# A two-block transformer kernel on one core: the second block's softmax heads in pairs, mirrored decay levels, meta keys' values over all rows

## The reference, cut to what matters

```python
# block 2, attention: 16 heads of 64; with 256 tokens it is one block, so plain causal softmax
q, k = rope(heads(q)), rope(heads(k))
s = einsum('bhqd,bhkd->bhqk', q, k) * 64 ** -0.5
p = softmax(where(k_pos <= q_pos, s, NEG))
o = einsum('bhqk,bhkd->bhqd', p, v)

# block 2, HGRN2: 8 heads, keys and values of 128, b = running sum of log(forget)
a[t, s] = sum_d q[t, d] * k[s, d] * exp(b[t, d] - b[s, d])      for s <= t
o = a @ v       # and RMSNorm by head, times silu(output gate)

# block 1, attention: two softmaxes a head over 272 keys, of which 16 are meta tokens
a = softmax(s0) - lam * softmax(s1);  o = a @ v
```

## Time and profile before

| | |
|---|---|
| median of 3 executions | 1184.91 us (1183.97 to 1189.07) |
| the profiled execution | 1187.4 us, its span 1185.8 us |
| busy in the span | PE 1141.6, DVE 719.4, ACT 600.0, POOL 649.5 us |
| mean granted TensorE clock | 0.985 of full speed |
| chain that ended last | PE 77%, DVE 11%, issue 6% |
| one heads2 iteration | 65.36 us |

### The profile page before, as it was taken

How to read it: one execution, slowest core, us unless ns; L and a number is a source line. 1 busy time by engine, 2 the same in 40 slices (tenths; PEclk the granted TensorE clock), 3 DMA queues, 4 the chain that set the end, 5 groups by cost and what they waited for, 6 DMA issues and landing times.

```text
span 1185.8 us, 24894 instructions
## 1 busy us (share of the span) xinstructions
PE 1141.6 (96%) x8962; PEld 1095.6 (92%) x8962; DVE 719.4 (61%) x1364; ACT 600.0 (51%) x1112; POOL 649.5 (55%) x451
## 2 busy tenths in 40 slices
PE   6999999999889999999899999999999999999997
PEld 6999999998779999999899989898999989999996
DVE  5675766688656777525875856757666546444322
ACT  5644444455255656437555455555535455444332
POOL 4666666660355666644763637364375436656542
PEclk9999999999889999998999999999999999999998
DMA  8444444341343454543433423333445425545531
GB/s 324 145 147 141 156 141 161 142 147 72 142 178 114 173 192 169 205 148 137 164 126 109 162 99 122 141 109 139 147 174 172 149 90 195 178 177 198 193 143 36
DMA packets 26209, 179.43 MB, mean 151 GB/s; under 512 B 2848, under 2 KB 4128, under 8 KB 4768
## 3 DMA queue, kind: packets, MB, share of 16 engines
q1 hardware_dynamic: 25856, 178.28, 42.2%
q10 hardware_dynamic: 288, 0.27, 0.1%
HBM read 177.49 MB, written 1.05 MB: 151 GB/s over the span
## 4 chain that ended last, share of the span: by engine, by line
PE 77%; DVE 11%; issue 6%; POOL 2%; ACT 2%; DVEq 0%; DMA 0%; POOLq 0%; ACTq 0%
PE ps L570 51%; PE ps L852 10%; PE ps L930 2%; POOL parts L415 2%; PE ps L636 1%; PE ps L485 1%; DVE ps L2185 1%; DVE act L1823 1%; PE ps L667 1%; PE ps L610 1%; DVE branch L1964 1%; PE ps L923 1%; ACT parts L1130 1%; DVE parts L415 1%; PE ps L533 1%
## 5 line engine op out<-in xcount | busy, mean ns | idle before, releaser
L415 POOL TENSOR_TENSOR parts<-ring,parts 128x1024 fp32r<-128x1024 f32 x208 | 513.5, 2479 | 478.2 <-ACT parts L1130 475.1
L570 PE MATMUL ps<-x_high,parts 128*128 128x256 f32 (+2 forms) x3088 | 417.4, 284 | 4.3 <-DVE glu L1999 2.2
L570 PEld LDWEIGHTS ps<-x_high,parts 128*128 128x128 f32 x3088 | 387.2, 189 | 15.1 <-issue 8.1
L1130 ACT ACTIVATE parts<-ring 128x1024 fp32r<-128x1024 f32 x324 | 323.9, 1049 | 138.5 <-PE ps L852 69.3
L415 DVE TENSOR_TENSOR parts<-ring,parts 128x1024 fp32r<-128x1024 f32 x116 | 151.8, 1309 | 127.3 <-ACT parts L1130 127.3
L570 PE MATMUL ps<-x_low,parts 128*128 128x256 f32 (+2 forms) x1520 | 214.5, 284 | 0.0
L570 PEld LDWEIGHTS ps<-x_low,parts 128*128 128x128 f32 x1520 | 196.3, 189 | 0.0
L1750 DVE SCALAR_TENSOR_TENSOR ps<-glu,table_sb,ps 128x256 f32<-128x256 f32 x232 | 93.3, 479 | 0.6 <-DVE ps L1750 0.2
L852 PE MATMUL ps<-act_high,parts 128*128 128x256 f32 x704 | 87.8, 280 | 0.0
L852 PEld LDWEIGHTS ps<-act_high,parts 128*128 128x128 f32 x704 | 85.1, 188 | 0.0
L570 PE MATMUL ps<-parts,x_high 128*128 128x256 f32 x448 | 62.3, 285 | 0.9 <-DVE work L2098 0.9
(11 more groups left out here) (331 smaller groups left out, 1611.0 us busy)
## 6 DMA issues: line engine op xcount, KB each, us to landing
ring<-weights SPq DMA_DIRECT2D x166, 1024.0 KB, 4.8
res<-h_in SPq DMA_DIRECT2D x4, 272.0 KB, 3.7
act<-mem SPq DMA_DIRECT2D x1, 1024.0 KB, 14.9
out<-xT SPq DMA_DIRECT2D x4, 256.0 KB, 2.5
table_sb<-table SPq DMA_DIRECT2D x1, 969.5 KB, 9.0
table_sb<-table ACTq DMA_DIRECT2D x1, 132.5 KB, 3.5
work<-positions ACTq DMA_DIRECT2D x1, 128.0 KB, 4.7
```

Of the source, the lines that this page charges most:

```text
L415: eng.tensor_tensor(parts[:, LOW - HIGH + p, cols], ring[:, slot, cols], parts[:, p, cols].bitcast(F32), ALU.subtract)\
L570: mm = pe.matmul(out, left(k), right(k), start=step_ == 0 and k == 0, stop=step_ == 2 and k == KB - 1)
L1130: sc.activation(parts[:, p, cols], ring[:, slot, cols], ACT.Copy).then_inc(split_high, 1)
```

## The change

**Softmax heads in pairs.** `scores2(s)`, `values2(s)`, `maxima2()`, `exps2()` and `turned2()` now each do two heads, one on either half of the array, with a second `p2` and `p2T` (where the other half of `kl` was). The pair's scores lie in banks 4 and 5, and their transposes go back to the same banks. The matmuls of the two halves alternate. The order of all three queues around them is changed: TensorE does both `turn2` behind `hgrn_scores(1, 0)`; VectorE does `maxima2` for both heads, then `low_v` of chunk 6, then both `normalise2`; ScalarE does `exps2` for both, then `ahead2(4)`. In the second pair VectorE has `low_values`, `level(13)` and `cross_level` between `maxima2` and `normalise2`, and ScalarE has `ahead2(5)` ahead of `decay(13)` and `cross_decay`, which stood ahead of it before.

**Mirrored levels.** The second half's tokens are kept in reverse order of keys, so that the keys of a level in the first half and those in the second take different rows of one 128 x 128 `kl`, and one matmul of 128 columns does both halves. VectorE multiplies the keys of each half by itself (64 columns each, the second written backwards). `iN`'s second half is reversed by a matmul with a reversed identity (`mirror_values`, 256 columns, between tiles 4 and 5) and copied back by ScalarE, which waits for it ahead of `decay(2)`; `head_keys` becomes four copies of half the width. The reversed identity and masks are made by VectorE in `down1` (`mirrored_constants`). GpSimd's clearing of `kl` falls away.

**Meta keys' values.** The matmul over the 16 meta keys takes all 128 rows, the others being cleared once at the start by GpSimd.

```diff
@@ TensorE
-                pe.matmul(ps[:, 7, 0:P], v_meta[0:META, h * P:h * P + P], a1M[0:META, :], start=True, stop=False)
+                pe.matmul(ps[:, 7, 0:P], v_meta[:, h * P:h * P + P], a1M, start=True, stop=False)
...
+            def mirror_values(i):
+                b = STREAM.bank("heads2", 3)
+                hold(pe, bank_read[2], n.before(bank_read[2]))
+                pe.wait_ge(tile_read[b], STREAM.before("heads2", i, 3) + 1)
+                pe.matmul(ps[:, 2, 0:CW], both_diagonals[:, P:2 * P], iN[:, 1, :], start=True, stop=True)\
+                  .then_inc(values_mirrored, 1)
+            def scores2(s):
...
+                for half in range(2):
+                    pe.matmul(ps[:, 4 + half, 0:P], q_r[rows[half], s, 0:P], k_r[rows[half], s, 0:P], start=True, stop=True)
+                for half in range(2):
+                    mm = pe.matmul(ps[:, 4 + half, P:3 * P], q_r[rows[half], s, P:SEQ], k_r[rows[half], s, :], start=True, stop=True)
...
             def level(h, l, bank, at):
-                for blk in range(2):
-                    mm = pe.matmul(ps[:, bank, at + HD * blk:at + HD * blk + HD], kl[:, l, blk * P:blk * P + P],
-                                   ql[:, l, blk * HD:blk * HD + HD], start=True, stop=True)
-                return mm
+                return pe.matmul(ps[:, bank, at:at + P], kl[:, l, :], ql[:, l, :], start=True, stop=True)
...
-                for t in range(6):
+                for t in range(5):
                     proj(t)
+                mirror_values(i)
+                proj(5)
...
                 scores2(0)
                 hgrn_values(0)
                 proj(10)
+                hgrn_scores(1, 0)
                 turn2(0)
-                scores2(1)
-                hgrn_scores(1, 0)
+                turn2(1)
                 proj(11)
                 values2(0)
-                turn2(1)
-                scores2(2)
+                scores2(1)
                 proj(12)
                 hgrn_scores(1, 1)
+                proj(13)
+                turn2(0)
+                turn2(1)
+                hgrn_scores(1, 2)
+                proj(14)
                 values2(1)
-                turn2(2)
-                scores2(3)
-                proj(13)
-                hgrn_scores(1, 2)
-                values2(2)
-                turn2(3)
-                proj(14)
                 hgrn_values(1)
-                values2(3)
                 proj(15)
@@ ScalarE, heads2
+                sc.wait_ge(values_mirrored, n.next(values_mirrored))
+                sc.activation(iN[:, 1, :], ps[:, 2, 0:CW], ACT.Copy).then_inc(bank_read[2], 1)
                 decay(2)
...
-                exps2(0)
+                exps2()
                 ahead2(4)
                 hgrn_output(i, 0)
                 copy2(10, gates[:, i * 2, 0:SEQ], fn=ACT.Tanh, scale=0.5)
                 turned2()
-                exps2(1)
                 for x in range(9, 13):
                     decay(x)
                 copy2(11, gates[:, i * 2 + 1, 0:SEQ], fn=ACT.Tanh, scale=0.5)
-                turned2()
-                exps2(2)
+                output2(i, 0)
+                exps2()
+                ahead2(5)
                 decay(13)
                 cross_decay(i, 1)
-                ahead2(5)
@@ VectorE, level and heads2
-                ve.tensor_tensor(halves(kl[:, l, :], m)[:, :, 0, :], halves(kh[:, i * 2 + h, :], m)[:, :, 0, :],
-                                 e[:, :, 0, :], ALU.mult)
+                ve.tensor_tensor(halves(kl[:, l, :], m)[:, :, 0, :], keys[:, 0:b, 0, :], e[:, 0:b, 0, :], ALU.mult)
+                ve.tensor_tensor(halves(kl[:, l, :], m)[:, ::-1, 1, ::-1], keys[:, b:, 0, :], e[:, b:, 0, :], ALU.mult)
...
-                maxima2(0)
-                normalise2()
+                maxima2()
                 low_v("heads2", i, 6)
-                maxima2(1)
-                normalise2()
+                normalise2(0)
+                normalise2(1)
                 gather0()
                 for x in range(9, 13):
                     level(i, 1, x)
-                maxima2(2)
-                normalise2()
+                maxima2()
+                low_values(i, 0)
                 level(i, 1, 13)
                 cross_level(i, 1)
-                low_values(i, 0)
+                normalise2(0)
+                normalise2(1)
                 low_v("heads2", i, 7)
-                maxima2(3)
-                normalise2()
```

More of the change, by code:

```diff
@@ L362, in blocks_kernel @@
         m_max, m_sum = small[0:LEAD, 16:32], small[0:LEAD, 32:48]
+        nmax2, rsum2, rden2 = (small[:, 16 + 4 * j:20 + 4 * j] for j in range(3))
         lb, one_lb, lb_t = small[:, 48:56], small[:, 56:64], small[:, 64:88]
@@ L895, in rotate @@
                           start=True, stop=True).then_inc(bank_full[2], 1)
[L897 to L900, removed]
-                    pe.wait_ge(roped, n.next(roped, 2))
[L902 to L905, removed]
@@ L907, in turn2 @@
-            def turn2(j):
+            def mirror_values(i):
[5 more added lines that the diff above has]
+            def scores2(s):
+                if s == 0:
+                    pe.wait_ge(roped, n.next(roped, 2))
+                hold(pe, bank_read[5], n.now(bank_read[5]))
+                rows = [slice(HD * half, HD * half + HD) for half in range(2)]
+                for half in range(2):
+                    pe.matmul(ps[:, 4 + half, 0:P], q_r[rows[half], s, 0:P], k_r[rows[half], s, 0:P], start=True, stop=True)
+                for half in range(2):
+                    mm = pe.matmul(ps[:, 4 + half, P:3 * P], q_r[rows[half], s, P:SEQ], k_r[rows[half], s, :], start=True, stop=True)
+                mm.then_inc(bank_full[4], 1)
@@ L908, in turn2, with values2 @@
+            def turn2(half):
+                n.before(bank_read[4])
+                n.before(bank_read[5])
                 pe.wait_ge(probs_ready, n.next(probs_ready))
-                hold(pe, bank_read[5], n.before(bank_read[5]))
                 for b in range(3):
-                    mm = pe.transpose(ps[:, 5, b * P:b * P + P], p2[:, b * P:b * P + P], ident)
+                    mm = pe.transpose(ps[:, 4 + half, b * P:b * P + P], p2[half][:, b * P:b * P + P], ident)
                 mm.then_inc(bank_full[5], 1)
[L914 to L917, removed]
+            def values2(s):
+                bank = VALUE_BANKS[s]
@@ L918, in values2 @@
                 hold(pe, bank_read[5], n.now(bank_read[5]))
[L919 to L926, removed]
+                hold(pe, bank_read[bank], n.before(bank_read[bank]))
@@ new lines, in values2 @@
+                for blk, queries in ((0, slice(0, SEQ)), (1, slice(P, SEQ))):
+                    for half in range(2):
+                        c = s * P + HD * half
+                        mm = pe.matmul(ps[HD * half:HD * half + HD, bank, queries], vA[:, blk, c:c + HD],
+                                       p2T[half][:, 0:SEQ] if blk == 0 else p2T[half][:, SEQ:SEQ + P],
+                                       start=blk == 0, stop=blk == 1, skip_group_check=True)
+                mm.then_inc(bank_full[8], 1)
@@ L1437, in head_keys, with exps2 @@
             def head_keys(i, h):
-                sc.activation(kh_s[:, h, :], kh[:, i * 2 + h, :], ACT.Copy).then_inc(khs_ready, 1)
-            def exps2(j):
-                sc.wait_ge(max_ready, n.next(max_ready, 2))
-                sc.activation(p2[:, 0:P], ps[:, 4, 0:P], ACT.Exp, bias=nmax[:, 0:1], accum_out=rsum[:, 0:1])
-                sc.activation(p2[:, P:3 * P], ps[:, 4, P:3 * P], ACT.Exp, bias=nmax[:, 1:2],
-                              accum_out=rsum[:, 1:2]).then_inc(bank_read[4], 1)
+                sc.activation(kh_s[:, h, 0:P], kh[:, i * 2 + h, 0:P], ACT.Copy)
+                sc.activation(kh_s[:, h, SEQ - 1:P - 1:-1], kh[:, i * 2 + h, P:SEQ], ACT.Copy).then_inc(khs_ready, 1)
+            def exps2():
+                for half in range(2):
+                    sc.wait_ge(max_ready, n.next(max_ready))
+                    sc.activation(p2[half][:, 0:P], ps[:, 4 + half, 0:P], ACT.Exp, bias=nmax2[:, half:half + 1],
+                                  accum_out=rsum2[:, half:half + 1])
+                    sc.activation(p2[half][:, P:3 * P], ps[:, 4 + half, P:3 * P], ACT.Exp, bias=nmax2[:, 2 + half:3 + half],
+                                  accum_out=rsum2[:, 2 + half:3 + half]).then_inc(bank_read[4], 1)
             def turned2():
-                sc.wait_ge(bank_full[5], n.next(bank_full[5]))
-                hold(sc, bank_full[8], n.now(bank_full[8]))
-                sc.activation(p2T, ps[:, 5, 0:3 * P], ACT.Copy).then_inc(bank_read[5], 1)
-                n.next(bank_full[8])
+                hold(sc, bank_full[8], n.before(bank_full[8]))
+                for half in range(2):
+                    sc.wait_ge(bank_full[5], n.next(bank_full[5]))
+                    sc.activation(p2T[half], ps[:, 4 + half, 0:3 * P], ACT.Copy).then_inc(bank_read[5], 1)
             def output2(i, s):
```

(16 more changed lines are left out.)

58 lines of the change are left out of this document (30 added, 28 removed).

## The result

The changed kernel took **1210.58 us** (median of 4 runs, 1209.5 to 1211.24), beside 1185.98 for the kernel before on the same chip: ratio 1.021, 95% interval 1.0191 to 1.0228. It is slower, by 24.6 us where 19.4 were forecast, and lies 6.6 us above the predicted 1204 and inside the range. It is nearer to the 1213 of the rival with a third collision than to the forecast's 1204, and the profile shows that collision.

What follows compares the result with a forecast made beforehand. TensorE's own stream was taken to bound heads2 (65.36 us an iteration); 4.85 saved against waits of 6.0 and 2.8 gave +14.6, with clock +6.4 and meta rows -1.6: +19.4, so 1204 us, range 1196 to 1211 (chance 0.45).

Steps and rivals of the forecast that it cites:

- third collision: Rival, chance 0.22: GpSimd starts chunk 5's low half before VectorE, which loses 2.1 us before the rotated keys; 1213 us.
- Savings of TensorE: heads2: TensorE's stream gets 4.85 us an iteration shorter, to 60.5 us if nobody waits.
- Levels: heads2: joining both halves into one matmul saves two records in each of 14 levels, 3.0 us an iteration.
- the 0.5: heads2: the added mirroring matmul, 256 fp32 columns, costs 0.45 us, with its start 0.5 an iteration.
- upper bound: heads2, an iteration: scores save 1.0 us, bounds 0 and 1.7; values save 0.95, bounds nothing and 1.6.
- The 30%: Share saved by alternating array halves, from four records in 0.45 us against 2 x 0.32; applied to scores and values.
- fewer visits of the half array: heads2: four fewer changes to the half array and back an iteration, about 0.1 us each, save 0.4.
- First new wait: heads2, first pair's probabilities: TensorE waits 5.3 + 0.4 us, 0.25 before the scores, 6.0 together; 3.85 if ports don't hold VectorE.
- Second new wait: heads2, second pair's probabilities: TensorE waits 2.4 + 0.4 = 2.8 us an iteration; 1.0 without the port.
- Clock: heads2: TensorE's clock falls behind the first wait, 1.6 us an iteration, +6.4 for four; nothing counted for the second wait.
- Meta rows: Meta keys' values at full rows save 16 x 0.2 = 3.2 us; half goes into an existing VectorE wait: -1.6.
- two rules of the Trainium skill: Weight loads overlap only across row groups (total about 4 us higher), or tiles load and run in parallel (about 2.5 lower).

Runs made afterwards that it cites:

- e5: The changed kernel with VectorE's low half of chunk 6, GpSimd's low half of chunk 5 and ScalarE's high copies of chunk 7 all later: 1169.16 us, ratio 0.9856.
- e9: e5 with the mirrored part taken back (full-width level keys, two matmuls a level): 1166.49 us, ratio 0.985 to the kernel before.
- e8: The kernel before with mirrored levels and meta rows, single heads, and GpSimd's low half of chunk 5 behind difference 9: 1184.35 us, ratio 0.9987.
- e1: The changed kernel with VectorE's low half of chunk 6 behind normalise2(1) instead of ahead of normalise2(0): 1193.49 us, ratio 1.0062 to the kernel before.
- e2: The changed kernel with GpSimd's low half of chunk 6 behind the differences 11 instead of ahead: 1203.65 us, ratio 1.0147 to the kernel before.
- e3: The changed kernel with GpSimd's low half of chunk 5 behind the difference 9 instead of ahead: 1202.46 us, ratio 1.0136 to the kernel before.
- e4: The changed kernel with ScalarE's high copies of chunk 7 behind decay 13 and cross_decay instead of ahead: 1196.58 us, ratio 1.0082 to the kernel before.
- e7: The kernel before with the mirrored levels and the meta rows, softmax one head at a time: 1191.84 us, ratio 1.0049.
- e6: The kernel before with only the meta keys' values over all 128 rows and the two clears: 1181.97 us, ratio 0.997.
- e10: e5 with values2 issuing all matmuls of one head, then the other's, instead of alternating: 1168.90 us, ratio 0.9868 to the kernel before.
- e11: e5 with scores2 issuing all of one head's scores, then the other's, instead of alternating: 1168.38 us, ratio 0.9856 to the kernel before.

## Why the prediction came out as it did

- **Savings of TensorE, 4.85 an iteration:** too small. e5, the same instructions with little waiting, is busy 59.81, so 5.5. Levels: 0.84 for four, 2.9 in all, as predicted (3.0). The mirror's start lies 0.24 us ahead of the next tile, but that tile takes 3.02 us where one behind another tile takes 2.85, so it costs 0.41, close to the 0.5. Scores 1.7 and values 1.6 are both at the upper bound. The 30% was misread from the earlier trace rows: its 0.45 us has the change back to the full array in it, 0.1, and what is left for two heads, 0.35, is what one would cost (0.32 x 144 / 128 = 0.36), so the row already showed a full overlap. The fewer visits of the half array are worth the rest of e9's 4.1, 0.8, not 0.4. The mirrored part should then save 2.9 - 0.4 = 2.5, and busy time fell by 2.3 (e8) and 1.4 (e5 against e9). Records beside a wait can't overlap with a next group: the four level records ahead of e5's first wait of the transposes are busy for 0.61 us, while in e8, without a wait there, the next tile starts 0.37 us behind their start. That this is all of the missing 1.1 us of e5 is not shown.
- **First new wait, 5.3 + 0.4 and 0.25 before the scores:** that of the transposes is right in place, cause and size (5.22 and the second half behind it). e1 shows the place, e2 the collision's share: 1.9, where 6.0 against 3.85 made it 2.15. The wait before the scores is 1.63, and with the third collision out of the way (e3) still 0.82, not 0.25.
- **Second new wait, 2.4 + 0.4:** right (2.33); e4 shows that the moved high copies make it.
- **Third collision:** this is the step that failed. It was given 0.22 as a rival that needs VectorE 0.35 us late, while the working itself had VectorE 0.9 us late by level 5. By its own numbers it was the likelier case, and belonged into the forecast. It costs 1.8 to 2.0 an iteration (e3), where the rival said 2.1, and the mirrored part alone brings it about (e7).
- **Clock, 1.6 an iteration:** the size of one dip was right (tile 14 takes 4.53 us in the changed kernel and 3.02 in e4), the count wrong. I took the only idle with rows, 2.76 us, and counted nothing for the second wait; the clock fell at it in three of the four iterations. Busy time is 2.2, 3.4 and 2.6 us above the 59.8 of e5 in the three windows.
- **Meta rows, -1.6:** about -3.6 (e6). A pair saves 0.36, not 0.2, and the wait behind took 2.3 of 5.8, not half.
- **Sum:** an iteration was to be 60.5 + 8.8 + 1.6 = 70.9, and the one shown is 59.8 + 10.2 + 3.4 = 73.4, the other two 1.2 and 0.8 less. The two misses, third collision and clock, are 2.0 and 1.8 of the 2.5; the larger savings gave 0.7 back and smaller waits the rest. By the profiles heads2 and what follows grew by 23.8 + 5.1 = 28.9 us where 21.0 were forecast, and the meta rows took 2 off that. So the total is near the forecast partly by luck: the third collision and the second dip were left out, and the savings and the meta rows were put too small.

## What to carry to other kernels

When an engine that never waits is made faster, look first at the queue of each engine that feeds it: here every saving was real, and three lines of order, each one a large subtraction or copy put in front of a short link of a chain, turned -17 us into +25. When the working shows that an engine will be late by more than the margin of a rival, that rival is the forecast. Cost each part of a change alone: the pairs were worth 4.1 us an iteration, the mirrored levels saved up to 2.3 on TensorE and gave as much back by making VectorE late.

## What was not expected of the hardware

- Matmuls on the two column halves of the array (128 rows, 64 columns each) run at the same time: 0.80 us for two heads, 0.79 for one. The same holds for the row halves (0.85 and 0.85). It does not hang on alternating them in the program (e10, e11). Of the two rules of the Trainium skill weighed in the prediction, the traces agree with its tiling page ("TensorEngine Tiling (Array Packing)", Key Properties) and not with the other: in the changed kernel a weight load of the second head starts at 699.21, while the first head's matmul of 699.15 runs for 0.43 us.
- An idle of 2.33 us is not always followed by the lower clock. In the changed kernel it was in three iterations (0.66 over the window from 711 shown) and not in the first, where the same wait ends at 637.97 and the window from 638 shows 1.00; nor in the kernel before, behind the 2.33 us idle that ends at 332.45 (1.00 from 332 to 337). Beside the waits of 5.2, and of 3.94 in e1, it fell each time; behind 1.63 us (the window from 682.6 to 688) it stayed at 1.00. The dips cost 2.2 to 3.4 us an iteration, so a price taken from one iteration can be off by a microsecond.
- Rows at the full 128 are cheaper than at 16: a pair with one matmul of 16 rows, and the change to it and back, costs 0.36 us more.
